# Outputs turned within the scores, casts behind the last exponentials, and a divided last scaling in a hybrid decoder step

## The reference, cut to what matters

```python
def branch_out(o_a, o_b, z_a, z_b, g_a, g_b, w_pa, w_pb, w_out):
    u_a = (o_a * jax.nn.silu(z_a)) @ w_pa
    u_b = (o_b * jax.nn.silu(z_b)) @ w_pb
    return (jax.nn.sigmoid(g_a) * u_a + jax.nn.sigmoid(g_b) * u_b) @ w_out

xp = xp + gate * branch_out(...)
y_prompt = rmsnorm(xp, g_final)      # y * rsqrt(mean(y*y) + eps) * g_final, per row of 2048
xs = xs + gate * branch_out(...)
y_sample = rmsnorm(xs, g_final)
```

## Time and profile before

| | us |
|---|---|
| runs: median (lowest to highest) | 3272.89 (3272.27 to 3274.21) |
| the profiled execution's own time | 3276.17 |
| its span | 3274.6 |
| PE busy | 3146.4 (96%) |
| DVE busy | 1703.6 (52%) |
| ACT busy | 755.9 (23%) |
| GpSimd (POOL) busy | 249.7 (8%) |
| mean granted TensorE clock | 0.986 of full |

### The profile page before, as it was taken

One profiled execution on the slowest core, in us unless ns is written; L12 is line 12 of the kernel. 1 busy time (PEld: TensorE's weight loads), 2 busy tenths in 40 slices (PEclk: granted clock), 3 DMA queues, 4 the chain that ended last, 5 costly groups with the idle time before them and its releaser, 6 DMA issues.

```text
span 3274.6 us, 52366 instructions
## 1 busy us (share of the span) xinstructions
PE 3146.4 (96%) x20707; PEld 2980.8 (91%) x20707; DVE 1703.6 (52%) x2401; ACT 755.9 (23%) x1214; POOL 249.7 (8%) x422
## 2 busy tenths in 40 slices
PE   5889999999999999999999999899989899999997
PEld 4769999999999999999999999667766899999997
DVE  4478888511332455545555455456544553654654
ACT  5230000011000111111111110443423333333332
POOL 3100000000000000000000000122113110010000
PEclk8999999999999999999999999999999999999998
DMA  9832222222222213223233234741259685584772
GB/s 314 281 115 80 66 85 66 72 66 72 59 78 59 92 59 114 76 86 116 72 105 97 85 91 133 216 111 55 84 148 304 197 273 136 188 254 122 211 208 76
DMA packets 523277, 419.28 MB, mean 128 GB/s; under 512 B 19868, under 2 KB 492188, under 8 KB 519900
## 3 DMA queue, kind: packets, MB, share of 16 engines
q1 hardware_dynamic: 501604, 339.48, 36.6%
q0 software_dynamic: 21568, 78.45, 6.5%
HBM read 345.28 MB, written 74.68 MB: 128 GB/s over the span
## 4 chain that ended last, share of the span: by engine, by line
PE 88%; DMA 4%; SPq 3%; DVE 2%; issue 1%; ACT 1%; POOL 0%; DVEq 0%; ACTq 0%; POOLq 0%
PE banks L282 18%; PE banks L284 18%; PE banks L283 18%; PE banks L1570 6%; PE banks L1572 6%; PE banks L1571 6%; PE banks L758 4%; PE banks L791 3%; PE banks L780 1%; PE banks L390 1%; DMA u_raw<-in_w_out 1%; SPq L922 1%; DMA pool_k<-in_cache_k 1%; DMA x_in<-in_x_prompt 1%; SPq L920 1%
## 5 line engine op out<-in xcount | busy, mean ns | idle before, releaser
L282 PE MATMUL banks<-h_hi,w_hi 128*128 128x352 f32 (+1 forms) x3552 | 1162.5, 327 | 0.0
L284 PE MATMUL banks<-h_hi,w_lo 128*128 128x352 f32 (+1 forms) x3552 | 1158.3, 326 | 0.0
L283 PE MATMUL banks<-h_lo,w_hi 128*128 128x352 f32 (+1 forms) x3552 | 1157.4, 326 | 0.0
L282 PEld LDWEIGHTS banks<-h_hi,w_hi 128*128 128x128 f32 x3552 | 666.9, 188 | 3.1 <-issue 3.0
L283 PEld LDWEIGHTS banks<-h_lo,w_hi 128*128 128x128 f32 x3552 | 669.2, 188 | 0.0
L284 PEld LDWEIGHTS banks<-h_hi,w_lo 128*128 128x128 f32 x3552 | 666.2, 188 | 0.0
L273 DVE TENSOR_TENSOR w_lo<-w_raw,w_hi 128x2048 fp32r<-128x2048 f32 (+1 forms) x78 | 177.7, 2278 | 645.1 <-ACT w_hi L268 521.7
L361 ACT ACTIVATE col<-banks 128x384 f32<-128x384 f32 x150 | 71.2, 475 | 1024.0 <-PE banks L284 984.4
L1625 DVE MAX8 best<-work 128x8 f32<-128x1088 f32 x224 | 289.3, 1292 | 10.1
L1627 DVE MATCH_REPLACE8 work<-best,work 128x1088 f32<-128x1088 f32 x224 | 285.9, 1276 | 0.0
L268 ACT CAST w_hi<-w_raw 128x2048 fp32r<-128x2048 f32 (+1 forms) x78 | 147.9, 1897 | 570.9 <-PE banks L284 520.5
(11 more groups left out here) (260 smaller groups left out, 3512.7 us busy)
## 6 DMA issues: line engine op xcount, KB each, us to landing
w_raw<-in_w_in SPq DMA_DIRECT2D x77, 1024.0 KB, 5.7
u_raw<-in_w_out SPq DMA_DIRECT2D x96, 512.0 KB, 5.4
scratch_proj<-col POOLq DMA_DIRECT2D x76, 544.0 KB, 3.0
ada_w<-in_w_ada SPq DMA_DIRECT2D x16, 2048.0 KB, 15.0
u_raw<-in_w_pb SPq DMA_DIRECT2D x48, 512.0 KB, 4.6
gate_w<-in_w_ada SPq DMA_DIRECT2D x16, 1024.0 KB, 7.7
u_raw<-in_w_pa SPq DMA_DIRECT2D x48, 256.0 KB, 3.3
gates<-scratch_proj SPq DMA_DIRECT2D x64, 192.0 KB, 2.5
```

What stands on the lines that cost most here:

```text
L282: nc.tensor.matmul(dst, w_hi[:, par, k, 0:width], h_hi[:, k, a:b], start=(k == 0), stop=False)
L283: nc.tensor.matmul(dst, w_hi[:, par, k, 0:width], h_lo[:, k, a:b], start=False, stop=False)
L284: mm = nc.tensor.matmul(dst, w_lo[:, par, k, 0:width], h_hi[:, k, a:b], start=False, stop=(k == KT - 1))
```

## The change

Seven edits:
1. `scores(n, outputs)`: in a step with a turn, `turn_outputs` is called behind the first product of the scores instead of ahead of the scores. Without scores (the last steps) it is called as before.
2. The three casts `higher_o(act, 0, g)` stand behind the copies of the last sequence (`last`) instead of those of sequence 6.
3. In the last chunk DVE multiplies the finished channels of `y_row` with `g_row` ahead of time (`gained`): channels 0 to 1023 of tile j in column 12 + j, channels 1024 to 1535 of the three tiles in column 15.
4. Behind the inverse root DVE scales the first 1536 channels of tile 0 by `rstd` (two parts), ACT those of tiles 1 and 2, and DVE scales and multiplies the last 512 channels of each tile.
5. SyncE (SP) stores the last chunk's rows in six parts (GpSimd before, in three); GpSimd stores the first two chunks.
6. In the last column of the last chunk PE turns column 14 behind 11 of the 16 channel groups of the product, instead of behind the product; columns 12 to 15 of the last chunk are written out.
7. DVE adds the rows of column 14 ahead of column 15's gate, instead of behind it.

```diff
-            def scores(n):
+            def scores(n, outputs):
...
                         mm = nc.tensor.matmul(dst, lhs, k_t[:, kh, key0 + a - at_col:key0 + b - at_col], start=True,
                                               stop=in_place(n))
+                        if outputs is not None:
+                            turn_outputs(outputs)
+                            outputs = None
...
                     turn_weights(m, 0)
-                if triple_due(n) is not None:
+                if n < NJ:
+                    scores(n, triple_due(n))
+                elif triple_due(n) is not None:
                     turn_outputs(triple_due(n))
-                if n < NJ:
-                    scores(n)
...
-                if isinstance(b, int) and b == NB - 2:
+                if last:
                     for g in range(3):
                         higher_o(act, 0, g)
...
+        TURN_AT = 11
+        GAINED = 12 * P
...
+            done = TT - 3
+            half = GAINED // 2
+            for x in range(2):
+                sp.wait_ge(y_norm, done + x + 1)
+                sp.dma_start(y_tiles[TT - 3][0][:, x * half:(x + 1) * half], y_row[:, 0, x * half:(x + 1) * half])\
+                    .then_inc(y_last, 16)
+            sp.wait_ge(y_scaled, 1)
+            sp.dma_start(y_tiles[TT - 2][0][:, 0:GAINED], y_row[:, 1, 0:GAINED]).then_inc(y_last, 16)
+            for j in range(2):
+                sp.wait_ge(y_norm, done + j + 3)
+                sp.dma_start(y_tiles[TT - 3 + j][0][:, GAINED:D], y_row[:, j, GAINED:D]).then_inc(y_last, 16)
+            sp.wait_ge(y_scaled, 2)
+            sp.wait_ge(y_norm, done + 5)
+            sp.dma_start(y_tiles[TT - 1][0], y_row[0:SMP, 2, :]).then_inc(y_last, 16)
+            sp.wait_ge(y_last, 16 * 6)
...
             root(NCH - 1)
+            act.wait_ge(y_rstd, NCH)
+            act.wait_ge(y_gained, 6)
+            for j in (1, 2):
+                t = TILES[NCH - 1][j]
+                part = y_row[0:ROWS_OF(t), j, 0:GAINED]
+                nc.scalar.activation(part, part, ACT.Copy, scale=rstd[0:ROWS_OF(t), t:t + 1]).then_inc(y_scaled, 1)
...
+            def gained(j, c0, c1):
+                rows = ROWS_OF(TILES[NCH - 1][j])
+                dve.wait_ge(small_in, 128)
+                dve.wait_ge(r_squared, KT * (NCH - 1) + c1)
+                part = y_row[0:rows, j, c0 * P:c1 * P]
+                nc.vector.tensor_tensor(part, part, g_row[c0 // 8][0:rows, c0 % 8 * P:(c1 - c0 // 8 * 8) * P], ALU.mult)\
+                    .then_inc(y_gained, 1)
...
+                    if first and 12 <= c < 15 and ch + 1 == NCH:
+                        gained(c - 12, 0, 8)
+                    if first and c == 15 and ch + 1 == NCH:
+                        for j in range(3):
+                            gained(j, 8, 12)
...
             add_rows(ch, KT - 3, 1)
+            add_rows(ch, KT - 2, 0)
             gated(ch, KT - 1, 1)
-            add_rows(ch, KT - 2, 0)
             add_rows(ch, KT - 1, 1)
             sum_rows(ch)
             inverse(ch)
-            for j in range(3):
-                normal(ch, j)
+            dve.wait_ge(y_gained, 6)
+            for x in range(2):
+                part = y_row[:, 0, x * (GAINED // 2):(x + 1) * (GAINED // 2)]
+                nc.vector.tensor_scalar(part, part, rstd[:, TILES[ch][0]:TILES[ch][0] + 1], None, ALU.mult)\
+                    .then_inc(y_norm, 1)
+            for j, t in enumerate(TILES[ch]):
+                rows = ROWS_OF(t)
+                part = y_row[0:rows, j, GAINED:D]
+                nc.vector.scalar_tensor_tensor(out=part, in0=part, scalar=rstd[0:rows, t:t + 1],
+                                               in1=g_row[1][0:rows, GAINED - D // 2:D // 2], op0=ALU.mult, op1=ALU.mult)\
+                    .then_inc(y_norm, 1)
...
+                    if isinstance(c, int) and c == KT - 1:
+                        three_passes(banks[:, 4 + par, 0:n], par, range(TURN_AT), n, m_hi, m_lo, whole=range(KT))
+                        turn(ch, c - 1, 1 - par)
+                        three_passes(banks[:, 4 + par, 0:n], par, range(TURN_AT, KT), n, m_hi, m_lo, whole=range(KT))\
+                            .then_inc(prod_done, 1)
+                        return
...
-                quads(pe, project, (0,))
+                quads(pe, project, (0, 3) if ch + 1 == NCH else (0,))
```

More of the change, by code:

```diff
@@ L1284, in decode_step @@
         y_stored = sem("y_stored")
+        y_gained = sem("y_gained")
+        y_scaled = sem("y_scaled")
+        y_last = sem("y_last")
+        TURN_AT = 11
+        GAINED = 12 * P
         w_pa, w_pb, w_out = ins["w_pa"][0], ins["w_pb"][0], ins["w_out"][0]
@@ L1385, in pool_merge @@
                     gated_o(ch + 1)
-                for j, t in enumerate(TILES[ch]):
-                    pool.wait_ge(y_norm, t + 1)
-                    pool.dma_start(y_tiles[t][0], y_row[0:ROWS_OF(t), j, :]).then_inc(y_stored, 16)
-            pool.wait_ge(y_stored, 16 * TT)
+                    for j, t in enumerate(TILES[ch]):
+                        pool.wait_ge(y_norm, t + 1)
+                        pool.dma_start(y_tiles[t][0], y_row[0:ROWS_OF(t), j, :]).then_inc(y_stored, 16)
+            pool.wait_ge(y_stored, 16 * 3 * (NCH - 1))
             pool.wait_ge(kv_stored, 16 * 10)
@@ L1561, in dve_merge, with three_passes @@
             inverse(ch)
-            for j in range(3):
-                normal(ch, j)
+            dve.wait_ge(y_gained, 6)
[3 more added lines that the diff above has]
+                    .then_inc(y_norm, 1)
+            for j, t in enumerate(TILES[ch]):
+                rows = ROWS_OF(t)
[3 more added lines that the diff above has]
+                    .then_inc(y_norm, 1)
         def pe_merge(pe, turn_outputs):
-            def three_passes(dst, par, ks, n, hi, lo, before=None):
+            def three_passes(dst, par, ks, n, hi, lo, before=None, whole=None):
                 for k in ks:
@@ L1569, in three_passes @@
                         before(k)
-                    nc.tensor.matmul(dst, u_hi[par][:, k, :], hi[:, k, 0:n], start=(k == ks[0]), stop=False)
+                    nc.tensor.matmul(dst, u_hi[par][:, k, :], hi[:, k, 0:n], start=(k == (whole or ks)[0]), stop=False)
                     nc.tensor.matmul(dst, u_hi[par][:, k, :], lo[:, k, 0:n], start=False, stop=False)
-                    mm = nc.tensor.matmul(dst, u_lo[par][:, k, :], hi[:, k, 0:n], start=False, stop=(k == ks[-1]))
+                    mm = nc.tensor.matmul(dst, u_lo[par][:, k, :], hi[:, k, 0:n], start=False,
+                                          stop=(k == (whole or ks)[-1]))
                 return mm
```

## The result

The changed kernel takes **3256.73 us** (median of 5 runs, 3249.25 to 3258.45) where the kernel before, run beside it, takes 3272.99 (5 runs, 3272.27 to 3275.33). The ratio is 0.9944, with a 95% interval of 0.9933 to 0.9956: 18 us less by the ratio, 16.3 by the medians. The profiled execution took 3257.73, with a span of 3256.2 us against 3274.6.

A forecast was written before the change was run, and what follows sets the result against it. TensorE was busy for 96% of the span, so edits pay only where it stands still or behind its last product. 6.5 - 1.7 + 0.8 + 0 + 2.6 = 8.2 us off the 3272.89 median gave 3264.7, range 3260.5 to 3269.3.

The forecast's parts named there:

- the turns: Attention: turning outputs behind the first score product puts that product into PE's wait; 0.8 us gained, ends -0.5 and +8.
- the last column: Last chunk's final column: three transposes delay the last product 0.4 us, but earlier row additions offset it; 0, ends -0.3 and +0.6.
- the casts: Seam before the merge: casts behind the last exponentials let the merge start 6.5 us sooner.
- the clock: Merge start: PE's new pause makes about 3.4 us of work run at half speed; 1.7 us lost, ends 0 and 3.4.
- The step that failed: End of span: the 7.2 us behind the last store's landing at 3267.4 hold nothing visible and stay unchanged.
- The divided scaling and the stores: Tail behind the inverse roots: last landing 2.6 us sooner, ends 0 and 4.6.
- the middle that I took between two sums: Tail: last landing at 3264.8, between 3265.4 with 1.1 us for the narrow last store and 3264.3 without it.
- The Trainium skill's price for a DMA: Tail: 2.0 us fixed plus bytes at 436 GB/s; as one stream, stores end near 3263.7 and the tail gains 3.7.
- The rival on the slower side: Tail: each store starts its bytes only after the previous one completes, six taking 20.6 us; 3276.2 us, chance 0.05.
- the rival of a held seam: Before the merge: a late load or PE's own chain holds the start, leaving only 0.8 + 2.6; 3269.5 us, chance 0.09.
- The rival of 10 us at half clock: Merge start: slow clock stays for 10 us and loses 5 us instead of 1.7; 3268.0 us, chance 0.17.
- The formula: Cost per turn: before, wait plus distance to values; after, larger of wait and first product plus larger of 1.35 and remaining distance.

The follow-up runs named there:

- Experiments 1: Kernel before, with the last three whole-tile stores issued by SyncE and GpSimd no longer waiting for them: 3264.09 us against 3274.05, ratio 0.9976.
- 2 (put back by one wait): Changed kernel, with GpSimd also waiting at its end for the six stores SyncE issued: 3261.6 us against 3274.05, ratio 0.9964.
- 3 (half hidden): Kernel before, GpSimd still issuing all stores but only SyncE waiting for the last three to land: 3268.98 us against 3273.84, ratio 0.9988.
- Experiment 8: Changed kernel without the divided scaling: DVE scales three whole tiles behind the roots, SyncE stores three parts; 3259.45 us against 3272.86, ratio 0.9958.
- experiment 4: Kernel before, with only the three casts moved behind the last sequence's exponentials: 3269.43 us against 3274.05, ratio 0.9983.
- experiment 5: Kernel before, with only the outputs turned within the scores, behind their first product: 3268.98 us against 3274.05, ratio 0.9985.
- experiment 6: Changed kernel, with the outputs turned behind the second key product of the scores instead of the first: 3260.93 us against 3272.86, ratio 0.9968.
- experiments 6 and 7: The second of these: changed kernel without the turning inside the last column, column 14 turned behind column 15's passes: 3258.58 us against 3273.84, ratio 0.995.

## Why the prediction was wrong

By the spans 18.4 us went, and 8.2 were forecast. In us, the 10.2 between them are: the stretch behind the last landing 6.8, the turns 2.3, the last column 0.4, the casts 0.2, the clock -0.4, and stretches that the change leaves alone 0.9.

- **The step that failed** is the sentence "The 7.2 us from there to the end of the span hold nothing that I can see, and I leave them as they are". They held GpSimd's closing drain, 6.85 us, and the change moves GpSimd's last instruction from the end of the kernel to 3079.8 us. I had noted that GpSimd no longer stores the last chunk and priced only when the stores are issued and land, not which engine is last to finish. The 7.2 us became 0.4. Experiments 1 (the drain moved away), 2 (put back by one wait) and 3 (half hidden) show it.
- **The divided scaling and the stores**: the last landing was to come 9.7 us behind the roots instead of 12.3, and it comes 9.7 behind. The sum inside it was luck in part. SyncE issued the last store at 4.35 us behind the start of the scaling, not at 2.9, since the last three stores took it 1.1 us each to issue (2.16 for two, then 1.14); the landing took 5.3. The forecast had 2.4 us of start and completion, 6.2 of data at 420 GB/s and up to 1.1 for the narrow last store. In the trace data moved from 3247.6 to 3255.4: 7.8 us, with 0.86 from the first issue to the first data and 0.36 from the last data to the last landing. The fixed part was 1.2 us smaller than taken and the data took 1.6 longer (436 GB/s early, 254 in the last window), and the middle that I took between two sums met the total. Experiment 8 puts the division alone at 1.8 us. The rest of the 2.6 comes with SyncE's stores: with whole tiles its last one lands 11.5 us behind the start of the scaling (4.2 us for this transfer), GpSimd's 12.2 (4.7). No table load, as taken. The Trainium skill's price for a DMA, weighed in the prediction, is one that its section gives for transfers issued by GpSimd, and these are SyncE's; it would have ended the stores 8.5 us behind the start of the scaling, 1.2 sooner than they ended; the price from the trace was nearer.
- **The rival on the slower side** (stores in series) did not happen: six stores, 2.62 MB, took 9.0 us from the first issue (3246.76) to the last landing.
- **The casts**: 6.5 forecast, 6.7 measured. Less the 5.2 us that the stages before had gained (the `qa` scores at 2540.9 instead of 2546.1), the steps come to casts from 2549.6, measured 2548.98, and merge at 2557.8, measured 2557.70. The casts came 0.6 us sooner and the way from them to the merge took 0.5 longer, which nearly cancel. Three subtractions and the weights' set the start, as argued, and the rival of a held seam did not happen.
- **The clock**: 1.7 forecast (0 to 3.4), 2.1 measured here, 2.7 in experiment 4, nothing in experiment 2. A mechanism that was right, with ends that were needed. The rival of 10 us at half clock did not happen: the merge ran slow from 2557.7 to 2562.6.
- **The turns**: the term was mis-sized, 0.8 against 3.1. The formula stood up where it was tried (two turns in experiment 5, the stage in experiment 6), but the pauses in it were 0.16 us too short each. Without that error block 4's loss of 0.17 a turn is gone: with the pause at 0.46 + 0.16 = 0.62 it is 0.62 + 1.58 = 2.20 before against 0.86 + 1.30 = 2.16 after. For the 14 moved turns of blocks 4 to 7 it is 14 x 0.16 = 2.2 us; with the 0.65 forecast for these blocks 2.9, against 2.6 measured. I had set as a mark of failure that the turns change the attention by more than 2 us, and they did.
- **The last column**: 0 forecast, less than 0.1 us by experiment 7.

The parts add up within the noise. By their ratios SyncE's stores alone bring 0.24%, the casts 0.17% and the turns 0.15%, each with 0.09% either way, 0.56% together, and the change has 0.56%; that the figures meet so closely is chance. By their own stages they bring 7.6, 2.9 and 2.9 us, and the divided scaling 1.8: 15.2 us, where the change has 16.3 by the medians and 18.4 by the two spans.

## What to carry to other kernels

Ask which engine ends last, not only which transfer: a span that goes on after the last landing with no work in any view is not empty, and in this kernel a GpSimd that waits for the last store costs 6.7 us more than a SyncE that does. When one takes a pause on TensorE from the profile and fills it with work priced by the distance between starts, the pause too must be taken from start to start. Where a group of operands is needed piece by piece, start the consumer on the first piece: it saved 2.5 us ahead of the merge here, and another 1.8 us since the clock did not fall at the merge's start.

## What the runs showed of the hardware that was not expected

- GpSimd's closing DRAIN took 6606 ns in the eight profiled executions in which none of its own transfers was near, 6851 in the three in which its own store had just landed, and 7895 in the one with its own store under way. SyncE's took 7 ns in every one. ScalarE's took 388 ns right behind a transfer of its own, 327 to 329 without one, and 3069 or 3071 where its two scalings still ran.
- SyncE needed 0.36, 0.36 and 0.44 us to issue its first three stores and 0.91, 1.21 and 1.14 us for the last three; a store issued 1.2 us earlier on a second queue landed no earlier.
- The granted clock fell to 0.50 around the start of the merge with PE pauses ahead of it of 3.33, 3.43, 3.77, 4.05 and 6.16 us (experiments 4 and 8, the changed kernel, experiments 6 and 7), and did not with one of 3.09 us in the same place (experiment 2). The five took 1.8 to 3.1 us more from the merge to `project` than experiment 2, and not in the order of their pauses.
- One stretch differs by up to 8 us from one profiled execution to another (129.9 to 137.9 us from the last turn to the last `qa` scores; PE's waits for the load of `pool_k` in it were 12.1 us in the longest and 7.7 in the shortest), and the medians of the kernel before went from 3272.86 to 3274.05. A part worth 2 us can hardly be read from the total. It can be read from one profile where its stage repeats: the time from the roots to the end, with the same stores, within 0.1 us, and columns 12 to 15 of the last chunk within 0.01. At the seam, which varies by over 1 us, it takes several.
